# Gathering the rows of an expert whole on 64 partitions, where they were gathered as halves on 128

## The reference

```python
def run(args):
    tok, e = args
    xb = t[tok]
    return (jax.nn.silu(xb @ e_gate[e]) * (xb @ e_up[e])) @ e_down[e]
```

## Time and profile before

| | |
|---|---|
| median of 3 runs | 1560.73 us (1553.86 to 1562.04) |
| the profiled execution | 1563.26 us, span 1561.4 us |
| PE busy | 1269.3 us, 81% of the span |
| VectorE, ACT, GpSimd busy | 544.0, 380.8 and 247.1 us |
| bytes moved | 358.46 MB, 230 GB/s over the span |
| expert stage of layer 0 | from some 525 to 845 us |
| expert stage of layer 1 | from some 1253 to 1523 us |

### The profile page before, as it was taken

The page is one execution under the profiler, slowest core; times in us unless marked ns, Lnnn a source line. Parts: engine busy times, 40 slices in busy tenths (PEclk is TensorE's granted clock), DMA queues, the critical chain, the costliest instruction groups (busy, mean ns, idle before and its releaser), DMA issues.

```text
span 1561.4 us, 16675 instructions
## 1 busy us (share of the span) xinstructions
PE 1269.3 (81%) x6542; PEld 735.4 (47%) x6542; DVE 544.0 (35%) x1160; ACT 380.8 (24%) x741; POOL 247.1 (16%) x265
## 2 busy tenths in 40 slices
PE   3799998977999599989784699888699678878770
PEld 1456465445345345546442465644555444444430
DVE  3325466455123432121002448453732510000006
ACT  3321124300123122122123501343014212211123
POOL 4210110001000123232221008100000022222220
PEclk9799999998998699999898699999899689999995
DMA  9736420054646599999997411202020769999965
GB/s 342 268 120 244 183 78 27 28 176 152 219 172 247 197 410 420 398 416 383 379 375 287 159 54 30 76 27 88 34 108 27 283 242 419 417 419 418 409 245 205
DMA packets 73521, 358.46 MB, mean 230 GB/s; under 512 B 13197, under 2 KB 22027, under 8 KB 37736
## 3 DMA queue, kind: packets, MB, share of 16 engines
q1 hardware_dynamic: 58012, 324.35, 53.6%
q0 software_dynamic: 12704, 22.03, 3.9%
q10 hardware_dynamic: 2732, 11.08, 1.8%
HBM read 340.32 MB, written 31.23 MB: 238 GB/s over the span
## 4 chain that ended last, share of the span: by engine, by line
PE 65%; DMA 12%; DVE 10%; ACT 6%; issue 5%; POOL 1%; ACTq 0%; SPq 0%; POOLq 0%; DVEq 0%
PE ps L1344 10%; PE ps L1292 9%; PE ps L1359 7%; DMA work<-h_scratch,tabs 5%; PE ps L1142 5%; PE ps L1052 4%; PE ps L913 3%; PE ps L1103 3%; PE ps L1073 2%; PE ps L1236 2%; DMA ring<-in_ada_w 2%; DMA mix_s<-in_exp_up 2%; PE ps L1351 1%; DMA fwd_s<-in_exp_down 1%; PE ps L966 1%
## 5 line engine op out<-in xcount | busy, mean ns | idle before, releaser
L1344 PE MATMUL ps<-ring,work 128*64 128x256 f32 x1312 | 158.0, 395 | 4.5 <-ACT work L1702 3.1
L1359 PE MATMUL ps<-ring,work 128*64 128x512 f32 x456 | 121.2, 655 | 36.4 <-DVE work L2218 17.0
L1292 PE MATMUL ps<-ring,yT 128*128 128x512 f32 x320 | 145.3, 604 | 2.0 <-DVE yT L2079 2.0
L2216 DVE TENSOR_TENSOR work<-work,ps 64x256 f32<-64x256 f32 x56 | 23.8, 424 | 326.9 <-ACT work L1709 326.9
L1344 PEld LDWEIGHTS ps<-ring,work 128*64 128x64 f32 x1312 | 103.1, 144 | 72.0 <-issue 30.8
L844 POOL DMA_INDIRECT work<-h_scratch,tabs x60 | 61.7, 1028 | 305.3 <-DVE tabs L2204 279.5
L849 POOL DMA_INDIRECT y_scratch<-work,tabs x56 | 57.5, 1028 | 324.2 <-ACT work L1716 324.2
L1957 DVE SCALAR_TENSOR_TENSOR work<-work,prmT 128x655 f32<-128x655 f32 x120 | 97.7, 901 | 0.0
L1292 PEld LDWEIGHTS ps<-ring,yT 128*128 128x128 f32 x320 | 59.7, 193 | 75.9 <-issue 73.7
L1142 PE MATMUL ps<-hT,ring 128*128 128x512 f32 x192 | 88.6, 604 | 1.1 <-DVE ring L1974 1.1
L913 PE MATMUL ps<-ring,c_act 128*32 128x512 f32 x384 | 59.0, 690 | 21.9 <-DMA ring<-in_ada_w 19.9
(11 more groups left out here) (375 smaller groups left out, 1960.5 us busy)
## 6 DMA issues: line engine op xcount, KB each, us to landing
ring<-in_exp_down SPq DMA_DIRECT2D x57, 1024.0 KB, 13.6
ring<-in_ada_w SPq DMA_DIRECT2D x48, 1024.0 KB, 4.8
ring<-in_exp_gate SPq DMA_DIRECT2D x41, 1024.0 KB, 10.8
ring<-in_exp_up SPq DMA_DIRECT2D x41, 1024.0 KB, 15.6
inv_s<-in_exp_gate SPq DMA_DIRECT2D x20, 1024.0 KB, 9.6
mix_s<-in_exp_up SPq DMA_DIRECT2D x20, 1024.0 KB, 15.2
ring<-in_w_in SPq DMA_DIRECT2D x16, 1024.0 KB, 7.7
fwd_s<-in_exp_down SPq DMA_DIRECT2D x11, 1024.0 KB, 19.6
```

The lines of the kernel that those rows point to most:

```text
L1292: last = mm(ps[:, (4, 6, 7, 0)[n % 4], :], yT[:, k, t * P:(t + 1) * P], wo[k // 2][:, k % 2, h * HALF:(h + 1) * HALF], start=(k == 0), sto ...
L1344: last = mm(ps[BR * q:BR * q + BR, 1, 0:FE], xe[:, s, kb, BR * h:BR * h + BR], w[q][:, k, :], start=(k == 0), stop=(k == KC - 1))
L1359: last = mm(ps[BR * h:BR * h + BR, 3, :], he[:, s, k, :], wd[:, k, HALF * h:HALF * h + HALF], start=(k == 0), stop=(k == 1))
```

## The change

Each place's row is gathered whole, 4 KB, on partitions 0 to 63, from `H_dram` with the token number as index. The two slots of `xg` are now two separate areas of 1024 columns on 64 partitions; the second shares its columns with `sg` and `hid`, which lie on the upper 64 partitions. `rows_in` transposes eight pieces of 64 rows by 128 channels, where it transposed four of 128 by 128, and `gate_up` reads piece `k` directly. The gather's part of the tables is the token number (one shift), where it was the half row's number (two shifts and the half). The scatter keeps its half rows. In the overflow loop PE increments an unused semaphore ahead of `rows_in`.

```diff
--- before.py
+++ after.py
@@ -222,8 +222,8 @@
         htok = at(work, 4096, 2, D)
         g2b = at(yflat, 3072, 2, D)
 
-        xg = at(work, 0, SLOTS, HALF)
-        xe = at(work, 1024, SLOTS, 4, 2 * BR)
+        xg = [at(work, 0, D)[0:BR, :], at(work, 6144, D)[0:BR, :]]
+        xe = at(work, 1024, SLOTS, KC, BR)
         ye = at(work, 2048, SLOTS, HALF)
         sg = at(work, 6144, SLOTS, FE)
         hid = at(work, 6656, SLOTS, FE)
@@ -842,8 +842,8 @@
 
                 def gather_rows(s, rows, done):
                     pool.indirect_dma_start(
-                        xg[:, s, :], None, H_half, bass.IndirectOffsetOnAxis(ap=rows.bitcast(U32), axis=0),
-                        bounds_check=2 * T - 1, oob_is_err=False).then_inc(done, 16)
+                        xg[s], None, H_dram, bass.IndirectOffsetOnAxis(ap=rows.bitcast(U32), axis=0),
+                        bounds_check=T - 1, oob_is_err=False).then_inc(done, 16)
 
                 def scatter_rows(s, rows, done):
                     pool.indirect_dma_start(
@@ -851,14 +851,14 @@
                         bounds_check=2 * T * TOPK - 1, oob_is_err=False).then_inc(done, 16)
 
                 for n in range(SLOTS):
-                    gather_rows(n, tabs[:, 0, n:n + 1], xg_in[n])
+                    gather_rows(n, tabs[0:BR, 0, n:n + 1], xg_in[n])
                 for n in range(NSTAT):
                     s = n % SLOTS
                     pool.wait_ge(xt_mm, nth(l, xt_mm, n + 1))
                     pool.wait_ge(xg_in[s], nth(l, xg_in[s], 16 * (n // SLOTS + 1)))
                     if n + SLOTS == NSTAT and l > 0:
                         pool.wait_ge(over_clear, l)
-                    gather_rows(s, tabs[:, 0, n + SLOTS:n + SLOTS + 1], xg_in[s] if n + SLOTS < NSTAT else d_xg[s])
+                    gather_rows(s, tabs[0:BR, 0, n + SLOTS:n + SLOTS + 1], xg_in[s] if n + SLOTS < NSTAT else d_xg[s])
                     pool.wait_ge(ye_ok, nth(l, ye_ok, n + 1))
                     scatter_rows(s, tabs[:, 1, n:n + 1], y_out[s] if n + SLOTS < NSTAT else d_yout[s])
                     if l + 1 < DEPTH:
@@ -880,7 +880,7 @@
                         pool.sem_inc(nop)
                         pool.wait_ge(d_xt, j * SLOTS + (s + 1))
                         pool.sem_inc(nop)
-                        gather_rows(s, icol[:, s, 0:1], d_xg[s])
+                        gather_rows(s, icol[0:BR, s, 0:1], d_xg[s])
                         pool.wait_ge(d_ye, j * SLOTS + (s + 2))
                         pool.sem_inc(nop)
                         scatter_rows(s, icol[:, s, 1:2], d_yout[s])
@@ -1331,17 +1331,16 @@
 
                 def rows_in(s):
 
-                    for k in range(4):
-                        last = tr(ps[:, 0, k * P:(k + 1) * P], xg[:, s, k * P:(k + 1) * P], ident)
+                    for k in range(KC):
+                        last = tr(ps[:, 0, k * BR:(k + 1) * BR], xg[s][:, k * P:(k + 1) * P], ident[0:BR, 0:BR])
                     return last
 
                 def gate_up(s, n):
 
                     w = [units[i].rearrange("p (k f) -> p k f", k=KC) for i in gu_units[l][gu_slot(l, n)]]
                     for k in range(KC):
-                        h, kb = k // 4, k % 4
                         for q in range(2):
-                            last = mm(ps[BR * q:BR * q + BR, 1, 0:FE], xe[:, s, kb, BR * h:BR * h + BR], w[q][:, k, :],
+                            last = mm(ps[BR * q:BR * q + BR, 1, 0:FE], xe[:, s, k, :], w[q][:, k, :],
                                       start=(k == 0), stop=(k == KC - 1))
                     return last
 
@@ -1412,6 +1411,7 @@
                             pe.wait_ge(d_xg[1], j * 16 + 16)
                         else:
                             pe.wait_ge(d_xg[0], j * 16 + 32)
+                        pe.sem_inc(nop)
                         rows_in(1 - s).then_inc(d_xt, 1)
                         pe.wait_ge(d_hm, i)
                         pe.sem_inc(nop)
@@ -1699,7 +1699,7 @@
                 act.wait_ge(ro_tab, l + 1)
 
                 def rows_out(s):
-                    return A(xe[:, s, :, :], ps[:, 0, :].rearrange("p (k t) -> p k t", k=4), ACT.Copy)
+                    return A(xe[:, s, :, :], ps[:, 0, :].rearrange("p (k t) -> p k t", k=KC), ACT.Copy)
 
                 act.wait_ge(xt_mm, nth(l, xt_mm, 1))
                 rows_out(0).then_inc(xe_ok, 1)
@@ -2199,10 +2199,10 @@
                 step(V.tensor_scalar(tabz[:, :], slots, 0.0, 8192.0, ALU.is_equal, ALU.mult))
                 step(V.scalar_tensor_tensor(out=tabf[:, :], in0=slots, scalar=-1.0, in1=tabz[:, :], op0=ALU.add, op1=ALU.add))
                 step(V.tensor_copy(tabi[:, 1, :], tabf[:, :]))
-                step(V.tensor_scalar(tabi[:, 0, :], tabi[:, 1, :], 1, 1, ALU.arith_shift_right, ALU.logical_shift_left))
+                V.tensor_scalar(tabs[:, 0, :], tabi[:, 1, :], 1, None, ALU.arith_shift_right)
                 step(V.tensor_scalar(tabi[:, 1, :], tabi[:, 1, :], 1, None, ALU.logical_shift_left))
-                V.tensor_tensor(tabs[:, :, :], tabi[:, :, :], halfi[:, 0:1].rearrange("p (a b) -> p a b", b=1)
-                                .to_broadcast([P, 2, NBLK + SLOTS]), ALU.bitwise_or).then_inc(ro_tok, 1)
+                V.tensor_tensor(tabs[:, 1, :], tabi[:, 1, :], halfi[:, 0:1].to_broadcast([P, NBLK + SLOTS]),
+                                ALU.bitwise_or).then_inc(ro_tok, 1)
 
                 dve.wait_ge(ro_exp, nth(l, ro_exp, 1))
                 step(V.tensor_reduce(gsum[:, :], gexp[:, :, :], AX.X, ALU.add))
```

## The result

The changed kernel took 1592.24 us (median of 4 runs, 1587.82 to 1593.89) against 1557.52 us for the kernel before on the same chip (4 runs, 1553.86 to 1562.04). The ratio is 1.0211, with an interval of 1.0181 to 1.0240. The forecast was 1573 us with a range up to 1587: the direction was right, the size too small by more than half.

What follows compares the result with a forecast made beforehand. It took weight transfers to bound the saturated stretches of the expert stages, and PE some of layer 0. Transposes +6.6, tables -0.4 and gathers +6.3 gave +12.5 us on the 1560.73 us median, so 1573 us, range 1558 to 1587.

Steps and rivals of the forecast that it cites:

- What bounds the kernel: Expert stages: weight transfers set the pace in saturated stretches at 417 to 419 GB/s, PE in some of layer 0.
- The transposes, +6.6 us: Row transposes on PE (L1335): eight narrow for four wide, +0.44 us at full clock, +0.90 at the lower one.
- The 0.88 and 1.8 us of the prediction: Forecast time of eight narrow transposes at L1335: 0.88 us at full clock, 1.8 at the start of a stage.
- The end that I had put below: Lower bound for the transposes at L1335: no growth, if the moving columns set the pace.
- The tables, -0.4 us: L2202 to L2204, ahead of each layer's first gather: one shift's wait gone, last operation halved; 0.2 us saved per layer.
- The gathers, +6.3 us: Row gathers (L844) to 64 partitions in saturated stretches: a third of 18.9 us for 49 gathers.
- the full price: Rival: each gather delays the weights by all its extra time, 0.386 us, 18.9 us in all; 1586 us, chance 0.16.
- the second rival: The full price: weights delayed for each gather's whole extra time, layer 1 at 398 GB/s, 1586 us, chance 0.16.
- The packets of the POOL queue: Sign: the POOL queue's packets fall by some 2560, one for each of 1280 pairs in two layers.
- Half the partitions cost nothing: Rival: weights keep 417 GB/s, because gathers are a twentieth of the bytes; 1567 us, chance 0.22.
- no cost: Rival: moving columns set the transposes' pace and half the partitions cost nothing, leaving only the tables; 1560 us, chance 0.10.
- Gathers land earlier: Rival: half as many packets land some 2 us sooner, removing 6.5 us of PE's gather waits; 1560 us, chance 0.10.

Runs made afterwards that it cites:

- e5: Changed kernel with whole rows gathered on partitions 32 to 95, places spread, and eight plain matmuls in place of the transposes; 1591.37 us, ratio 1.0212.
- e10: Changed kernel with whole rows on partitions 32 to 95 in the kernel's own order, read by eight transposes over all 128 partitions; 1565.45 us, ratio 1.0063.
- e8: Changed kernel with all indices of the stage's gathers out of bounds, so they move nothing; 1539.26 us, ratio 0.9893 to the kernel before.
- e11: Kernel before with all indices of the stage's gathers out of bounds, so they move nothing; 1541.42 us, ratio 0.9912.
- e1: Changed kernel with the second slot's rows gathered on partitions 64 to 127, so the slots alternate between the halves; 1591.91 us, ratio 1.0210.
- e6: Kernel before plus one plain POOL-queue load a turn, 128 pieces of 1280 bytes, to partitions 0 to 63; 1621.39 us, ratio 1.0404.
- e12: Kernel before plus the extra load of e6, but to partitions 32 to 95; 1582.49 us, ratio 1.0156.
- e7: Kernel before plus the extra load of e6, but to all 128 partitions; 1580.97 us, ratio 1.0149.
- e13: Kernel before plus the extra load of e6 as 64 pieces of 2560 bytes, to partitions 0 to 63; 1619.84 us, ratio 1.0405.
- e14: Kernel before plus half the extra load of e6, 64 pieces of 1280 bytes, to partitions 0 to 63; 1589.63 us, ratio 1.0217.
- e15: Kernel before plus the half load of e14, but to partitions 32 to 95; 1569.14 us, ratio 1.0072.
- e3: Kernel before with the places of each set of 64 rows permuted, so filled rows are spread over the partitions; 1549.01 us, ratio 0.9920.
- e9: Changed kernel with whole rows on partitions 32 to 95, places spread, read by eight transposes over all 128 partitions; 1548.15 us, ratio 0.9947.
- e4: Kernel of e1, slots on alternating halves, with the places of each set of rows also permuted; 1586.51 us, ratio 1.0172.
- e2: Changed kernel with the places of each set of 64 rows permuted; 1586.65 us, ratio 1.0190 to the kernel before.

## Why the prediction was wrong, step by step

*What bounds the kernel* held: the transfers set the pace in the saturated stretches, and a loss of rate there is paid about one for one: layer 1's 246.8 us, from its first gather to the overflow gather, times 417 / 387 are 266, and 267.3 were measured.

*The transposes, +6.6 us, failed; the growth is nothing that the runs can tell.* PE's timeline of the kernel after in layer 1, beside the earlier trace rows:
```profile
...
1308.05 0.71 PE L1335 MATMUL ps<-sq,work 64*128 64x64 f32 x8
1309.05 0.45 PE L1350 MATMUL ps<-sq,work 64*128 64x64 f32 x2 [0.29 <-DVE work L2216]
...
```
Eight take 0.71 us where four took 0.65, and at the start of layer 1's stage, at the lower clock, 1.09 us as the four did (1264.62 and 1257.11 above). The 0.88 and 1.8 us of the prediction had their price from L982 and L1328. These are plain matmuls, not transposes, and the trace records each of them twice: L982's four as x8, L1328's ten as x20, the transposes once each. They also load 128 rows, the new transposes 64. So "loading sets the pace" was read from another kind of instruction: e5's eight plain matmuls over 128 rows took 2.0 us, e10's eight transposes over 128 rows 1.09. The end that I had put below, no growth, is what came; its reason, that the moving columns set the pace, is not shown, as the rows loaded and the columns moved were halved together. e8 and e11 say the same for the whole run.

*The tables, -0.4 us,* came as forecast, too small to matter: from the start of L2202 to the end of L2204 it is 0.53 us, where the earlier trace rows gives 0.72.
```profile
...
518.73 0.19 DVE L2202 TENSOR_SCALAR tabs<-tabi 128x54 int32<-128x54 int32 x1
...
519.04 0.22 DVE L2204 TENSOR_TENSOR tabs<-tabi,halfi 128x54 int32<-128x54 int32 x1
...
```

*The gathers, +6.3 us, is the term that was mis-sized: it measured some 36 us (49.5 less 13.7).* The mechanism, that 64 partitions from 0 hold up the transfers, was the right one, read from the earlier trace rows. Two choices made the term small. First, I took a third of the full price, because the mean load of the lower partitions stayed under a rate that had been seen. e1 shows that a mean over a turn is the wrong measure: each gather makes its own dip. Second, the full price itself was too low. What the engines moved in 1300 to 1460 us, before and then after:
```profile
...
DMA packets 11532, 66.84 MB, mean 418 GB/s; under 512 B 2616, under 2 KB 2616, under 8 KB 4126
...
```
```profile
...
DMA packets 10685, 62.24 MB, mean 389 GB/s; under 512 B 2405, under 2 KB 2405, under 8 KB 3775
...
```
The 4.60 MB that are missing take 11.0 us at 418 GB/s, 0.58 us for each of the 19 gathers, beside the 0.386 us that the doubling gives. So the rate fell below the second rival's 398. By the same sum e6 against e12 loses 0.75 us for each of 18 loads of 0.164 MB. A byte for one half then costs 2.5 to 2.9 times a byte across both, not twice.

The prediction counted only the gather's own bytes at half the rate. Most of the loss is in the packets of the weights: SP's queue was busy 90.8% of 1280 to 1480 us for 75.40 MB before and 90.0% for 69.87 MB after, 7% more time per MB. In 1300 to 1460 us its packets of 8 KB took 315 ns on average before, 338 after and 313 in e10; half of them took no longer than before (312 and 313 ns), but the slowest tenth took over 441 ns, where it had been 321. Of the packets' extra time some four fifths are the weights', one fifth the POOL queue's. Why it adds up to more than twice stays open, and so does whether the weights' packets wait for the partitions of the busy half or for the DMA engines that serve them: the traces don't tell the engines apart. The Trainium skill, "SBUF — State Buffer", section "Door 1: The DMA port swizzle (why `[64,N]` ≈ `[32,N]`)", says that adding 32 to a partition keeps its port and adding 64 changes it, by which partitions 32 to 95 reach all 16 ports; e10 and e12 agree, at 419 and 415 GB/s, and its factor of two is exceeded here.

A rest stays: 49 gathers, as the prediction counted them, at 0.58 us are 28 us, and the two stages lost 33.9. The prediction had counted the gathers of two windows, where 70 sets of rows are gathered in all; how the rest is divided among them was not measured.

*The packets of the POOL queue* did not fall by 2560. The page has 12704 in both kernels; here are the line of the kernel after and that of e6, whose 56 loads of 128 pieces add 2688 packets, 48 each:
```profile
...
q0 software_dynamic: 12704, 22.02, 4.3%
...
```
```profile
...
q0 software_dynamic: 15392, 31.21, 5.7%
...
```
A packet of the profile is not a piece of the program: most bytes of the POOL queue go in packets of 4096 bytes, 5252 of them before and 5282 after. 7.90 MB / 4000 was no size of a piece.

*The rivals.* "Half the partitions cost nothing" and "no cost" fell with the rate. "Gathers land earlier" fell with the landing of 8.0 us. "The full price" was nearest, 1586 us, and reached its sum with 6.2 us for transposes that weren't there.

## What to carry to other kernels

Where transfers are the bound, look at which partitions a small transfer fills: here 64 partitions from 0 cost over twice the bytes' time, and 64 from 32 cost no more than 128. Bound a burst by what it does while it lasts, and not by its mean over a turn. If an experiment's time says no, read the rate of the stretch before giving the theory up: e5 had cured the transfers and paid for it on PE.

## What the runs showed of the hardware that was not expected

- A plain load costs 6.9 to 7.4 us per MB on partitions 0 to 63 and 2.4 to 2.6 on 32 to 95 or on all 128, beside a stream of weights that fills the DMA engines (e6, e7, e12 to e15).
- Eight transposes of 64 rows into 64 columns take 0.71 us, and eight of 128 into 128 take 1.09 us, at full clock. Eight plain matmuls with 128 rows loaded and 64 columns moved take 2.0 us (e5).
- Permuting the places within a set of rows alone was worth 0.8% in the kernel before (e3), 1.2% between e10 and e9, 0.4% between e1 and e4, yet nothing clear in the kernel after (e2). That it spreads the filled rows over the DMA engines is argued, not shown.
